# Gated DeltaNet layers of a decoder trunk: order of the inverse's matmuls, place of two sample updates, and the engine that scales one group of query products

## The chip, the cores and the metric

The program runs on one NeuronCore of one Trainium2 chip. Its engines are TensorE (PE in the profile, with PEld for its weight loads), VectorE (DVE), ScalarE (ACT), GpSimd (POOL) and SyncE (SP, which issues DMAs). Each engine works through its own list of instructions in the order in which it was written, and waits at semaphores for the others. The metric is the time of one execution on the device in microseconds (us), median of the runs.

## The reference, cut to what matters

The reference runs a prompt of 256 tokens and a decode batch of 8 sequences with 4 tokens each through four layers. Every layer has a half-step SwiGLU FFN, a token mixer and another half-step FFN. Layers 0 and 3 have a gated DeltaNet mixer with 8 heads of 128; the change lies in it alone. For the prompt it works in four chunks of 64 tokens:

```
a_mat = eye + (kb @ kc^T) * decay_strict          # 64 x 64 for each head and chunk
u, w  = solve(a_mat, [v * beta, kb * exp(gc)])    # unit lower triangular
step(S):  v_new = u_n - w_n @ S                   # four steps, one after the other
          o     = qg_n @ S + attn_n @ v_new
          S     = S * gl_n + kdec_n^T @ v_new
o = rmsnorm(o) * silu(z);  y = o @ w_out
```

The samples have a state of their own for every sequence and head, 8 x 8 matrices of 128 x 128, which gets `S * gl + kdec^T @ v_new` once.

## The kernel before

Everything is float32. Big projections are done as three passes of rounded halves (lines 412 to 414 and 1275 to 1277); the small products of the mixer are plain float32 matmuls. The eight heads are two groups `g` of four, the four chunks two tiles `p` of 128 tokens with two halves `e`. There is no scheduler: each engine's order is written out by hand, and the order of the source is the order of issue. `once(engine, "name", v)` makes an engine wait until the named semaphore has reached v; `.then_inc` raises it when the instruction is done.

**The inverse.** `pe_gdn` inverts the triangular matrices by levels. Level l is `inverse_z(pe, l)` (L1438, 64 matmuls of 64 x 64 into `ZBANK`), then VectorE's `masked_z(l)` (L1998, two instructions), `inverse_x(pe, l)` (L1453, 64 matmuls) and VectorE's `x_turned(l)` (L2004, two transposes) beside ScalarE's `xt_copy`. Each waits for the one before. Between them TensorE does other work: `turned(pe, t)` for t = 0 to 7 turns one tile of keys (t even) or values (t odd) into a bank of PSUM (L1395 for group 0, L1398 for group 1), `sample_small(pe, k)` (L1466, 16 small matmuls) and `sample_old(pe, n, g)` (L1479). VectorE's `k_scaled(t)` (L2016) and ScalarE's `v_scaled(t)` (L1687) read what was turned. All `turned` raise one semaphore, `g_t`.

**The recurrence.** `chain(pe, c)`, c = 0 to 3, is one chunk step: the product of w and S (L1555); VectorE subtracts it from u (L2128, two instructions, `g_y`); the product of q and S (L1566, `g_qs`), which ScalarE scales into `O` (`q_scaled`, L1783, four instructions a group, `g_qe`); the product of the attention and v_new (L1579), which VectorE adds to `O` (L2141, `g_o`); and `chain_state` (L1594), the state's product, which VectorE adds to S (L2120).

**The samples' states.** The 16 updates k = 0 to 15 are products of one 32-row strip each with 512 columns (`sample_update`, L1542). Strip k % 4 is used. Updates 0 to 3 have four PSUM banks, 0, 1, 2 and 6; from k = 4 on `update_bank` is k % 2, so bank 0 or 1. An even update is added to the state by VectorE (`updated(k)`, L2090, raises `g_s_new`). An odd one is copied to `fbuf` by ScalarE (`update_copied(k)`, L1775, raises `g_ssu_copied`) and added by GpSimd (L1186, raises `g_s_odd`). From k = 4 on update k waits first for its bank:

```
once(pe, ("g_s_new", "g_ssu_copied")[k % 2], k // 2)
```

which is `updated(k - 2)` for an even k and `update_copied(k - 2)` for an odd one. In step c > 0 TensorE sends updates 4c and 4c + 1 behind the product of q and S, and 4c + 2 and 4c + 3 at the end of the step.

**The end of the recurrence.** TensorE sends `outputs_turned` 0 to 3 (L1608, L1611), 14 matmuls whose result nobody reads (`pe_filled`, L494), `outputs_turned` 4 and 5, 12 more such matmuls, and then the output projection (L1275). VectorE takes means of squares (`mean(2)`, L2095), gates what was turned (`gated`, L2103, in the order 0, 2, 4, 1, 3, 5) and makes the low parts (`low`, L2110). ScalarE squares (L1755), takes the root (`root(2)`, L1759 and L1760), scales group 0 of `O` (`normed(1, 0)`, L1799) and makes the high parts (`hi`, L1769). `gated(0)` writes where `update_copied(13)` had put its copy, so it waits for seven adds of GpSimd (`g_s_odd`). The projection starts when the low parts 0, 2 and 4 are there.

Of the kernel before, what the change touches and what calls it, by code (L numbers as in the profile page):

```python
# [19 lines left out]
ALU = mybir.AluOpType  # L20
# [37 lines left out]
def tables():  # L58
# [53 lines left out]
    for b in range(NB):  # L112
# [18 lines left out]
        g_evac=14, g_silu=12, g_sq=8, g_ss_half=1, g_act_seq=4, g_lnp=1, g_alog=1, g_egl=1, g_lk=1, g_ce=1, g_trow_ready=2, g_dt=2,  # L131
        g_dts=1, g_tv=4, g_x=10, g_s_x=1, g_s_xt2=1, g_s_y=1, g_ue=4, g_qe=4, g_ms=5, g_ro=3, g_on=3, g_on_d=1, g_on_p=2, g_o_hi=6,
        g_dve_seq=14, g_hist_in=10, g_tap=12, g_tapped=24, g_z_in=4, g_hist=1, g_cbuf_half=2, g_cbuf_set=1, g_conv=12, g_tail=12, g_gate_read=2, g_abs=1, g_gl=1,
        g_rows=2, g_egx=1, g_ssr=1, g_colc=1, g_tabr=1, g_e=1, g_m2=2, g_xt=4, g_tk=4, g_s_xt=1, g_s_kv=2, g_s_r=1, g_s_rhs=1,
# [85 lines left out]
def trunk(nc, a, subs):  # L220
# [29 lines left out]
    def once(eng, name, v):  # L250

        eng.wait_ge(sem(name), v + before(name))

    with ctx:
# [819 lines left out]
        o_cols = lambda k: slice(k * P, (k + 1) * P) if k < 2 else slice(0, 4 * P)  # L1074
        DBANK, KQBANK, ZBANK, XTBANK = ((2, 3), (4, 5)), (6, 7), (2, 6), (7, 3)
        TBANK, UBANK, WBANK = (1, 5, 4, 5, 1, 5, 4, 5), ((2, 4), (3, 7)), ((5, 6), (0, 2))
        SUBANK, QSBANK, AYBANK, OBANK = (4, 5), (2, 6), (3, 7), (2, 2, 4, 6, 3, 7)
# [127 lines left out]
        def pe_gdn(pe, n):  # L1205
# [23 lines left out]
            inverse_z(pe, 2)  # L1229
            sample_turned(pe)  # L1230
            inverse_x(pe, 2)
            sample_small(pe, 0)
            turned(pe, 0)
            turned(pe, 1)
            inverse_z(pe, 3)
            sample_small(pe, 1)
            turned(pe, 2)
            turned(pe, 3)
            inverse_x(pe, 3)
            sample_small(pe, 2)  # L1240
            turned(pe, 4)
            turned(pe, 5)
# [138 lines left out]
        def turned(pe, t):  # L1381

            g, p, v = t // 4, t // 2 % 2, t % 2
            if t == 0:
                once(pe, "g_s_kv", 1)
                once(pe, "g_silu", 12)
            elif t < 3:
# [12 lines left out]
            last.then_inc(sem("g_t"), 1)  # L1400
# [144 lines left out]
        def chain(pe, c):  # L1545

            p, e = c // 2, c % 2
            if c == 0:
                once(pe, "g_ue", 4)
                once(pe, "g_we", 2)  # L1550
            else:
                once(pe, "g_s", 2 * c)
                for hh in range(4):
                    for g in range(2):
                        last = pe.matmul(psum[halves(e ^ g), SUBANK[g], hh * P:(hh + 1) * P], WT[:, g, e, 2 * hh + p, :],  # L1555
                                         S[:, 4 * g + hh, :], start=True, stop=True)
                        if hh == 3:
                            last.then_inc(sem("g_ws"), 1)
                if c == 1:
                    once(pe, "g_s_new", 2)  # L1560
                    once(pe, "g_ssu_copied", 2)
                elif c == 2:
                    once(pe, "g_qe", 2)
                for hh in range(4):
                    for g in range(2):
                        last = pe.matmul(psum[halves(e ^ g), QSBANK[g], hh * P:(hh + 1) * P], q4[:, 0, 4 * g + hh, chunk(p, e)],  # L1566
                                         S[:, 4 * g + hh, :], start=True, stop=True)
                        if e == 1 and hh == 3:
                            last.then_inc(sem("g_qs"), 1)
                sample_update(pe, range(4 * c, 4 * c + 2))  # L1570
                once(pe, "g_y", 2 * c)
# [13 lines left out]
            if c == 3:  # L1585
                chain_state(pe, c)
            sample_update(pe, range(4 * c + 2 * (c > 0), 4 * c + 4))

# [10 lines left out]
        def outputs_turned(pe, k):  # L1599

            p, g = (None, None, 0, 0, 1, 1)[k], k % 2
            if k == 0:
                once(pe, "g_qe", 4)
            elif k == 2:
                once(pe, "g_s", 7)
            once(pe, ("g_on", "g_on", "g_on_p", "g_on_p", "g_on", "g_on_d")[k], (1, 2, 1, 2, 3, 1)[k])
            if p is None:
# [6 lines left out]
        def act_gdn(act, n):  # L1614
# [67 lines left out]
            def v_scaled(t):  # L1682
                g, p = t // 4, t // 2 % 2
                once(act, "g_t", t + 1)
                for hh in range(4):
# [91 lines left out]
            def q_scaled(p):  # L1777
                for g in range(2):
                    once(act, "g_qs", 2 * p + g + 1)
# [44 lines left out]
            q_scaled(1)  # L1824
            update_copied(13)
            squared(1, 0, whole=False)
            squared(1, 1, heads=range(2))
            root(2, slice(8, 16))
            normed(1, 0)
            update_copied(15)  # L1830
            for k in OUT_ORDER:
# [39 lines left out]
        def dve_gdn(dve, n):  # L1871
# [139 lines left out]
            def k_scaled(t):  # L2011
                g, p = t // 4, t // 2 % 2
                once(dve, "g_t", t + 1)
                cols = slice(8 * p + 4 * g, 8 * p + 4 * g + 4)
                for k, dst in ((1, Kb), (2, KD)):
# [32 lines left out]
            dve.tensor_tensor(RHS, two(psum[:, 1, 256:512]), sc(0), ALU.mult).then_inc(sem("g_s_kv"), 1)  # L2048
            x_turned(2)
            masked_z(3)  # L2050
# [3 lines left out]
            once(dve, "g_conv_out", 128)  # L2054
            k_scaled(0)
            x_turned(3)
            k_scaled(2)
            masked_z(4)
# [63 lines left out]
            for c in range(4):  # L2122
                p, e = c // 2, c % 2
                if c > 0:
                    for g in range(2):
                        once(dve, "g_ws", 2 * (c - 1) + g + 1)
                        yv = U[halves(e ^ g), g, p]
                        dve.tensor_tensor(yv, yv, four(psum[halves(e ^ g), SUBANK[g], :]), ALU.subtract).then_inc(sem("g_y"), 1)  # L2128
                    updated(4 * c)
                if c < 3:  # L2130
# [5 lines left out]
                if e == 1:  # L2136
                    for g in range(2):
                        once(dve, "g_ay", 2 * p + g + 1)
                        once(dve, "g_qe", 2 * p + g + 1)
                        rows = slice(0, P) if p else halves(1 - g)  # L2140
# [11 lines left out]
            once(dve, "g_zs", 4)  # L2152
            mean(2, slice(8, 16))
            updated(14)
            state_added(3, 1)
# [1707 lines left out]
```

## Time and profile before

| | us |
|---|---|
| median of 3 runs | 2508.9 (2507.91 to 2509.67) |
| the profiled execution: its own time | 2510.39 |
| its span, first to last instruction | 2508.7 |
| TensorE busy | 2484.8 (99%) |
| VectorE busy | 1566.8 (62%) |
| ScalarE busy | 1187.4 (47%) |
| GpSimd busy | 313.5 (12%) |
| mean granted TensorE clock | 0.999 |

Starts are counted from the first instruction of the span. A row of a timeline has the start, the length of the merged piece, the engine, the line, what is written and read, how many instructions were merged, and in brackets the idle time before them and what ended it. The length of a piece of TensorE runs to the modelled end of its last matmul, so the next piece often starts a little before it; the distance from start to start is the time that a piece takes of the engine.

### The profile page before, as it was taken

Reading aid. Unit: us, or ns where it says so; the run is one execution under the profiler, and the core shown is the slowest. Engines: PE = TensorE matmul, PEld = TensorE weight load, DVE = VectorE, ACT = ScalarE, POOL = GpSimd, SP = SyncE. Lnnn points to the kernel's source line nnn. Section 1 sums busy time; section 2 is a strip of 40 time slices with the busy share of each in tenths; the row PEclk is TensorE's granted clock in tenths of the full one; section 3 lists DMA queues with packets and bytes.
Section 4 is the critical chain, followed back from the end, with each engine's and each line's share of the span. In section 5 each row is a group of like instructions: output and inputs, shape, how many; then the busy total and the mean of one; then the engine's idle time right before and its main releaser. Section 6 shows DMA issues by size and latency. Waiting matters only on the chain.

```text
span 2508.7 us, 49685 instructions
## 1 busy us (share of the span) xinstructions
PE 2484.8 (99%) x20967; PEld 2391.4 (95%) x20967; DVE 1566.8 (62%) x1956; ACT 1187.4 (47%) x1622; POOL 313.5 (12%) x336
## 2 busy tenths in 40 slices
PE   9999999999999999999999999999999999999999
PEld 9999988999999987799999999999999999979999
DVE  5556977755665556575465556675566549867654
ACT  5434755544544455454354444453454437555443
POOL 1001025100100155010010010110020011061000
PEclk9999999999999999999999999999999999999999
DMA  7546535444554657354455465555454466345543
GB/s 226 167 139 179 170 91 171 158 163 143 181 167 142 194 167 223 120 164 159 150 179 167 143 186 185 159 181 163 143 186 162 138 183 172 99 134 169 167 143 112
DMA packets 425365, 404.16 MB, mean 161 GB/s; under 512 B 27996, under 2 KB 420824, under 8 KB 424888
## 3 DMA queue, kind: packets, MB, share of 16 engines
q1 hardware_dynamic: 420568, 392.44, 50.1%
q0 software_dynamic: 4480, 9.18, 1.2%
q8 instruction: 129, 2.11, 0.4%
q14 instruction: 44, 0.36, 0.0%
q10 hardware_dynamic: 144, 0.07, 0.0%
HBM read 385.25 MB, written 16.39 MB: 160 GB/s over the span
## 4 chain that ended last, share of the span: by engine, by line
PE 96%; DVE 2%; issue 1%; ACT 1%; DMA 0%; SPq 0%; DVEq 0%; ACTq 0%
PE psum L412 25%; PE psum L413 25%; PE psum L414 25%; PE psum L750 2%; PE psum L754 2%; PE psum L751 2%; PE psum L3235 1%; PE psum L3248 1%; PE psum L3274 1%; PE psum L1542 1%; PE psum L532 0%; PE psum L507 0%; PE psum L1453 0%; PE psum L1438 0%; PE psum L1579 0%
## 5 line engine op out<-in xcount | busy, mean ns | idle before, releaser
L392 DVE TENSOR_TENSOR w_lo<-raw,w_hi 128x2048 fp32r<-128x2048 f32 (+3 forms) x361 | 742.8, 2058 | 492.4 <-ACT w_hi L375 491.8
L412 PE MATMUL psum<-xn_hi,w_hi 128*128 128x288 f32 x3296 | 974.1, 296 | 0.9 <-issue 0.4
L413 PE MATMUL psum<-xn_lo,w_hi 128*128 128x288 f32 x3296 | 973.3, 295 | 0.0
L414 PE MATMUL psum<-xn_hi,w_lo 128*128 128x288 f32 x3296 | 969.9, 294 | 0.0
L375 ACT ACTIVATE w_hi<-raw 128x2048 fp32r<-128x2048 f32 (+2 forms) x349 | 597.5, 1712 | 771.8 <-PE psum L414 756.9
L412 PEld LDWEIGHTS psum<-xn_hi,w_hi 128*128 128x128 f32 x3296 | 621.3, 189 | 6.9 <-issue 4.4
L414 PEld LDWEIGHTS psum<-xn_hi,w_lo 128*128 128x128 f32 x3296 | 620.1, 188 | 0.0
L413 PEld LDWEIGHTS psum<-xn_lo,w_hi 128*128 128x128 f32 x3296 | 619.4, 188 | 0.7
L413 PE MATMUL psum<-h_lo,w_hi 128*128 128x288 f32 x1408 | 415.5, 295 | 0.0
L414 PE MATMUL psum<-h_hi,w_lo 128*128 128x288 f32 x1408 | 414.9, 295 | 0.0
L412 PE MATMUL psum<-h_hi,w_hi 128*128 128x288 f32 x1408 | 413.2, 293 | 0.0
L414 PEld LDWEIGHTS psum<-h_hi,w_lo 128*128 128x128 f32 x1408 | 264.7, 188 | 0.0
L412 PEld LDWEIGHTS psum<-h_hi,w_hi 128*128 128x128 f32 x1408 | 264.7, 188 | 0.0
L413 PEld LDWEIGHTS psum<-h_lo,w_hi 128*128 128x128 f32 x1408 | 264.6, 188 | 0.0
L473 POOL TENSOR_TENSOR fbuf<-sq 128x576 f32<-128x576 f32 x21 | 42.9, 2041 | 1578.6 <-ACT sq L780 1375.7
L889 ACT ACTIVATE h_hi<-fbuf 128x576 f32 (+1 forms) x88 | 60.4, 687 | 207.2 <-DVE fbuf L953 207.2
L926 DVE TENSOR_TENSOR sg<-psum,rr 128x576 f32<-128x576 f32 x81 | 61.4, 757 | 154.5 <-PE psum L414 153.3
L956 DVE TENSOR_TENSOR h_lo<-fbuf,h_hi 128x576 f32 (+1 forms) x88 | 66.8, 759 | 81.0 <-ACT h_hi L889 81.0
L477 POOL TENSOR_TENSOR fbuf<-fbuf,sq 128x576 f32<-128x576 f32 x30 | 66.7, 2223 | 142.2 <-ACT sq L780 139.6
L1907 DVE SCALAR_TENSOR_TENSOR g_cacc<-g_cbuf,vec,g_cacc 128x312 f32<-128x312 f32 x144 | 73.8, 554 | 1.7
L953 DVE TENSOR_TENSOR fbuf<-sg,fbuf 128x576 f32<-128x576 f32 x88 | 66.2, 752 | 5.0 <-DVE fbuf L946 4.4
L927 DVE TENSOR_TENSOR fbuf<-psum,rr 128x576 f32<-128x576 f32 x81 | 60.6, 748 | 0.0
(673 smaller groups left out, 2906.9 us busy)
## 6 DMA issues: line engine op xcount, KB each, us to landing
raw<-w_ffn_up SPq DMA_DIRECT2D x175, 1024.0 KB, 5.1
raw<-w_ffn_down SPq DMA_DIRECT2D x64, 768.0 KB, 4.5
raw<-w_ffn_down SPq DMA_DIRECT2D x64, 640.0 KB, 4.2
raw<-gdn_w_in SPq DMA_DIRECT2D x32, 1024.0 KB, 5.6
raw<-mlstm_w_in SPq DMA_DIRECT2D x12, 1024.0 KB, 5.4
raw<-gdn_w_out SPq DMA_DIRECT2D x8, 1024.0 KB, 5.3
raw<-cache_mla_latent SPq DMA_DIRECT2D x36, 128.0 KB, 3.7
a_split<-cache_mla_latent SPq DMA_DIRECT2D x36, 128.0 KB, 3.2
```

The source lines that it names most:

```text
L375: act.activation(spread(w_hi[slot(u, i)], u), packed(raw[u % NRAW], u), ACT.Copy).then_inc(hi_ready, 1)
L392: dve.tensor_tensor(spread(w_lo[slot(u, i)], u), packed(raw[u % NRAW], u), spread(w_hi[slot(u, i)], u).bitcast(F32), ALU.subtract).then_in ...
L412: pe.matmul(out, wh[:, k, c], hi(k), start=st, stop=False)
L413: pe.matmul(out, wh[:, k, c], lo(k), start=False, stop=False)
L414: last = pe.matmul(out, wl[:, k, c], hi(k), start=False, stop=sp_)
L477: pool.tensor_tensor(sq_part, sq_part, sq[:, 2 * i:2 * i + 2, :], ALU.add).then_inc(sum_step, 1)
L889: act.activation(dst, fbuf[:, j % 2], ACT.Copy).then_inc(hhi_done, 1)
L926: dve.tensor_tensor(sg[:, j % 2], psum[:, s:s + 2, 0:T], r2, ALU.mult).then_inc(gate_ready, 1)
L927: dve.tensor_tensor(fbuf[:, j % 2], psum[:, s + 2:s + 4, 0:T], r2, ALU.mult).then_inc(pair_read, 1)
L953: dve.tensor_tensor(fbuf[:, j % 2], sg[:, j % 2], fbuf[:, j % 2], ALU.mult).then_inc(h_done, 1)
L956: dve.tensor_tensor(h_lo[:, sl, :], fbuf[:, j % 2], h_hi[:, sl, :].bitcast(F32), ALU.subtract).then_inc(hlo_done, 1)
L1907: last = stt(out=dst, in0=cbuf[:, i % 2, k, j:j + CW - 3], scalar=vec[:, r:r + 1], in1=dst, op0=ALU.mult, op1=ALU.add)
```

## The change

In the inverse, `turned(1)` is sent before `turned(0)`, and both, `turned` 2, 3 and 4, and `sample_small` 0 and 1 get other places between the levels. `k_scaled` and `v_scaled` ask for a tile's place in the new order, `k_scaled(0)` comes before `masked_z(3)`, `k_scaled(2)` before `x_turned(3)`, and the wait for the sum of the silus moves from `turned(0)` to `turned(1)` and `turned(2)`. In the last step of the recurrence TensorE sends updates 12 and 13 together with 14 and 15, behind `chain_state`; `updated(12)` goes behind `mean(2)` and `update_copied(13)` behind `normed(1, 0)`; and group 1 of the query products is scaled by VectorE in one instruction instead of by ScalarE in four. `sample_update` itself, with its banks and waits, is not touched.

```
+        TURN_ORDER = (1, 0, 2, 3, 4, 5, 6, 7)
 ...
             inverse_z(pe, 2)
             sample_turned(pe)
+            sample_small(pe, 0)
+            turned(pe, 1)
             inverse_x(pe, 2)
-            sample_small(pe, 0)
             turned(pe, 0)
-            turned(pe, 1)
+            turned(pe, 2)
+            sample_small(pe, 1)
             inverse_z(pe, 3)
-            sample_small(pe, 1)
-            turned(pe, 2)
             turned(pe, 3)
+            turned(pe, 4)
             inverse_x(pe, 3)
             sample_small(pe, 2)
-            turned(pe, 4)
             turned(pe, 5)
             inverse_z(pe, 4)
 ...  turned(pe, t)
             if t == 0:
                 once(pe, "g_s_kv", 1)
+            elif t < 3:
                 once(pe, "g_silu", 12)
-            elif t < 3:
                 once(pe, "g_dt", 2)
 ...  chain(pe, c)
-                sample_update(pe, range(4 * c, 4 * c + 2))
+                if c < 3:
+                    sample_update(pe, range(4 * c, 4 * c + 2))
                 once(pe, "g_y", 2 * c)
 ...
             if c == 3:
                 chain_state(pe, c)
-            sample_update(pe, range(4 * c + 2 * (c > 0), 4 * c + 4))
+            sample_update(pe, range(4 * c + 2 * (c in (1, 2)), 4 * c + 4))
 ...  outputs_turned(pe, k)
             if k == 0:
-                once(pe, "g_qe", 4)
+                once(pe, "g_qe", 3)
             elif k == 2:
                 once(pe, "g_s", 7)
+            elif k == 3:
+                once(pe, "g_o", 4)
 ...  v_scaled(t) on ScalarE, and the same in k_scaled(t) on VectorE
-                once(act, "g_t", t + 1)
+                once(act, "g_t", TURN_ORDER.index(t) + 1)
 ...  q_scaled(p)
-                for g in range(2):
+                for g in range(2 - p):
 ...  ScalarE's order
             q_scaled(1)
-            update_copied(13)
             squared(1, 0, whole=False)
             squared(1, 1, heads=range(2))
             root(2, slice(8, 16))
             normed(1, 0)
+            update_copied(13)
             update_copied(15)
 ...  VectorE's order in the inverse
             x_turned(2)
+            once(dve, "g_conv_out", 128)
+            k_scaled(0)
             masked_z(3)
 ...
-            once(dve, "g_conv_out", 128)
-            k_scaled(0)
+            k_scaled(2)
             x_turned(3)
-            k_scaled(2)
             masked_z(4)
 ...  VectorE's order in the recurrence
-                    updated(4 * c)
+                    if c < 3:
+                        updated(4 * c)
+                if c == 3:
+                    once(dve, "g_qs", 4)
+                    step(dve.tensor_tensor(O[:, 1, 1], four(psum[:, QSBANK[1], :]), CE[:, 3, 12:16, None].to_broadcast([P, 4, P]),
+                                           ALU.mult))
 ...
-                        once(dve, "g_qe", 2 * p + g + 1)
+                        once(dve, "g_qe", 3 if p else g + 1)
 ...
             mean(2, slice(8, 16))
+            updated(12)
             updated(14)
             state_added(3, 1)
```

## Rows read from the trace of the kernel before

**Rows 1.** The page's part 4: the chain that ended last, by engine.
```profile
PE 96%; DVE 2%; issue 1%; ACT 1%; DMA 0%; SPq 0%; DVEq 0%; ACTq 0%
```

**Rows 2.** Timeline of TensorE, layer 3, last step of the recurrence and after.
```profile
2249.14 1.13 PE L1542 MATMUL psum<-g_ym,y 32*128 32x512 f32 x4
2250.20 1.09 PE L1579 MATMUL psum<-g_u,g_m 64*64 64x128 f32 x16
...
2252.32 1.13 PE L1542 MATMUL psum<-g_ym,y 32*128 32x512 f32 x4
2253.37 0.44 PE L1608 MATMUL psum<-base,g_xn 128*128 128x128 f32 x2
...
2254.44 2.09 PE L494 MATMUL psum<-w_hi 128*128 128x288 f32 x14
2256.37 0.60 PE L1611 MATMUL psum<-base,g_o 128*128 128x128 f32 x4
...
2259.72 0.37 PE L1275 MATMUL psum<-xn_hi,w_hi 128*128 128x288 f32 x1 [0.36 <-DVE xn_lo L2110]
```

**Rows 3.** Timeline of VectorE, the same stretch.
```profile
2248.37 1.40 DVE L2128 TENSOR_TENSOR g_u<-g_u,psum 64x512 f32<-64x512 f32 x2 [0.33 <-PE psum L1555]
2250.30 0.69 DVE L2090 TENSOR_TENSOR y<-y,psum 128x512 f32<-128x512 f32 x1 [0.53 <-PE psum L1542]
2251.32 1.28 DVE L2141 TENSOR_TENSOR g_o<-g_o,psum 128x512 f32<-128x512 f32 x2 [0.33 <-PE psum L1579]
...
2254.16 0.17 DVE L2095 SCALAR_TENSOR_TENSOR g_ms<-g_ms,g_qe 128x8 f32<-128x8 f32 x1
...
2255.47 0.34 DVE L2103 SCALAR_TENSOR_TENSOR fbuf<-psum,vec,g_z 128x128 f32<-128x128 f32 x1
...
2257.01 0.75 DVE L2103 SCALAR_TENSOR_TENSOR g_ft<-psum,vec,g_z 128x512 f32<-128x512 f32 x1
```

**Rows 4.** Timeline of ScalarE, the same stretch.
```profile
2249.31 2.18 ACT L1783 ACTIVATE g_o<-psum,g_ce 128x128 f32<-128x128 f32 x8 [0.98 <-PE psum L1566]
...
2254.85 1.29 ACT L1799 ACTIVATE g_o<-g_o,g_ro 128x128 f32<-128x128 f32 x4
2256.04 0.58 ACT L1775 ACTIVATE fbuf<-psum 128x512 f32<-128x512 f32 x1
```

**Rows 5.** Timeline of GpSimd, the same stretch.
```profile
2252.05 1.28 POOL L1186 TENSOR_TENSOR y<-y,fbuf 128x512 f32<-128x512 f32 x1 [0.15 <-ACT fbuf L1775]
```

**Rows 6.** Timeline of TensorE, layer 3, step 0: four updates in a row.
```profile
2233.25 1.14 PE L1542 MATMUL psum<-g_ym,y 32*128 32x512 f32 x8
```

**Rows 7.** Timeline of TensorE, layer 3, the solved products.
```profile
2219.72 1.96 PE L1519 MATMUL psum<-g_vb,g_xt 64*64 64x128 f32 x32 [0.35 <-DVE g_xt L2009]
...
2224.55 0.84 PE L1498 MATMUL psum<-sq,g_xts 32*32 32x128 f32 x16 [0.93 <-DVE sq L2077]
2225.32 3.39 PE L1519 MATMUL psum<-g_vb,g_xt 64*64 64x128 f32 x32
```

**Rows 8.** Windows: busy time of each engine, PEclk (granted clock), DMA share.
```profile
2226.00:2228.00 2.00, 2.00 (x24) 2.00 (x22) 0.00 (x0) 0.60 (x1) 2.00 (x2) 0.50 0.03 11
```

**Rows 9.** Timeline of TensorE, layer 0, the inverse.
```profile
356.41 1.16 PE L1453 MATMUL psum<-g_xt,fbuf 64*64 64x64 f32 x64 [0.61 <-DVE fbuf L1998]
...
357.76 1.09 PE L1395 MATMUL psum<-base,g_qkv 128*128 128x128 f32 x8
358.96 1.16 PE L1438 MATMUL psum<-g_x,g_b 64*64 64x64 f32 x64
...
361.23 0.25 PE L1466 MATMUL psum<-g_xs,g_bs 32*32 32x32 f32 x3 [0.86 <-issue]
...
369.17 1.15 PE L1453 MATMUL psum<-g_xt,fbuf 64*64 64x64 f32 x61 [0.20 <-issue]
...
373.17 0.68 PE L1438 MATMUL psum<-g_x,g_b 64*64 64x64 f32 x29 [0.23 <-issue]
```

**Rows 10.** Timeline of VectorE, layer 0, the inverse.
```profile
357.59 1.31 DVE L2004 STREAM_TRANSPOSE g_x<-psum 128x512 f32<-128x512 f32 x2 [0.67 <-PE psum L1453]
```

More of the change, by code:

```diff
@@ L1230, in pe_gdn @@
             sample_turned(pe)
+            sample_small(pe, 0)
+            turned(pe, 1)
             inverse_x(pe, 2)
-            sample_small(pe, 0)
             turned(pe, 0)
-            turned(pe, 1)
+            turned(pe, 2)
+            sample_small(pe, 1)
             inverse_z(pe, 3)
-            sample_small(pe, 1)
-            turned(pe, 2)
             turned(pe, 3)
+            turned(pe, 4)
             inverse_x(pe, 3)
             sample_small(pe, 2)
-            turned(pe, 4)
             turned(pe, 5)
@@ L1385, in turned @@
                 once(pe, "g_s_kv", 1)
+            elif t < 3:
                 once(pe, "g_silu", 12)
-            elif t < 3:
                 once(pe, "g_dt", 2)
@@ L1569, in chain @@
                             last.then_inc(sem("g_qs"), 1)
-                sample_update(pe, range(4 * c, 4 * c + 2))
+                if c < 3:
+                    sample_update(pe, range(4 * c, 4 * c + 2))
                 once(pe, "g_y", 2 * c)
@@ L1586, in chain @@
                 chain_state(pe, c)
-            sample_update(pe, range(4 * c + 2 * (c > 0), 4 * c + 4))
+            sample_update(pe, range(4 * c + 2 * (c in (1, 2)), 4 * c + 4))
         def chain_state(pe, c):
@@ L1602, in outputs_turned @@
             if k == 0:
-                once(pe, "g_qe", 4)
+                once(pe, "g_qe", 3)
             elif k == 2:
                 once(pe, "g_s", 7)
+            elif k == 3:
+                once(pe, "g_o", 4)
             once(pe, ("g_on", "g_on", "g_on_p", "g_on_p", "g_on", "g_on_d")[k], (1, 2, 1, 2, 3, 1)[k])
@@ L1683, in v_scaled @@
                 g, p = t // 4, t // 2 % 2
-                once(act, "g_t", t + 1)
+                once(act, "g_t", TURN_ORDER.index(t) + 1)
                 for hh in range(4):
@@ L1777, in q_scaled @@
             def q_scaled(p):
-                for g in range(2):
+                for g in range(2 - p):
                     once(act, "g_qs", 2 * p + g + 1)
@@ L1824, in act_gdn @@
             q_scaled(1)
-            update_copied(13)
             squared(1, 0, whole=False)
@@ L1829, in act_gdn @@
             normed(1, 0)
+            update_copied(13)
             update_copied(15)
@@ L2012, in k_scaled @@
                 g, p = t // 4, t // 2 % 2
-                once(dve, "g_t", t + 1)
+                once(dve, "g_t", TURN_ORDER.index(t) + 1)
                 cols = slice(8 * p + 4 * g, 8 * p + 4 * g + 4)
@@ L2049, in dve_gdn @@
             x_turned(2)
+            once(dve, "g_conv_out", 128)
+            k_scaled(0)
             masked_z(3)
@@ L2053, in dve_gdn @@
                               gt("slevel")[:, None, :].to_broadcast([P, 2, NS]), ALU.mult).then_inc(sem("g_s_r"), 1)
-            once(dve, "g_conv_out", 128)
-            k_scaled(0)
+            k_scaled(2)
             x_turned(3)
-            k_scaled(2)
             masked_z(4)
@@ L2128, in dve_gdn @@
                         dve.tensor_tensor(yv, yv, four(psum[halves(e ^ g), SUBANK[g], :]), ALU.subtract).then_inc(sem("g_y"), 1)
-                    updated(4 * c)
+                    if c < 3:
+                        updated(4 * c)
+                if c == 3:
+                    once(dve, "g_qs", 4)
+                    step(dve.tensor_tensor(O[:, 1, 1], four(psum[:, QSBANK[1], :]), CE[:, 3, 12:16, None].to_broadcast([P, 4, P]),
+                                           ALU.mult))
                 if c < 3:
@@ L2153, in dve_gdn @@
             mean(2, slice(8, 16))
+            updated(12)
             updated(14)
```

7 lines of the change are left out of this document (4 added, 3 removed).

## The prediction

> **What bounds the kernel now.** I read the chain that ended last first. TensorE is 96% of it [rows 1], so a time changes only where TensorE comes to wait, loses a wait, or runs at a lower clock. Then the timelines of TensorE around the two places of the change, and those of VectorE, ScalarE and GpSimd for what releases it. The last step of the recurrence is gapless on TensorE up to the output projection, which waits 0.36 us for VectorE's low part [rows 2]. The inverse has short waits, for VectorE and for nothing that the profile shows ("issue") [rows 9]. Layers 0 and 3 run the same code, so each cost counts twice; the tail of layer 0 has the same distances as that of layer 3.
>
> **The last step: updates 12 and 13 moved.** Their place was 2249.14 to 2250.20, 1.06 us, beside VectorE's subtraction, 2248.37 + 1.40 = 2249.77 [rows 2, 3]. The attention product needs that subtraction. With the updates gone it can start 0.1 after 2249.77 instead of at 2250.20, 0.33 earlier. VectorE's add came 1.12 after it (2250.20 to 2251.32), and all up to `mean(2)` (2254.16) hangs on that add, so `mean(2)` comes at 2253.83.
>
> What stands behind this is the point of the forecast. Four updates are now in a row at the end, but `sample_update` keeps its two banks: update 14 waits for `updated(12)`, update 15 for `update_copied(13)`. The change puts `updated(12)` behind `mean(2)` on VectorE and `update_copied(13)` behind `normed(1, 0)` on ScalarE. TensorE keeps its order, so `outputs_turned` 0 to 3, the 14 unread matmuls, `outputs_turned` 4 and 5 and the projection queue up behind update 15. Step by step, in the times of layer 3:
> - `updated(12)`: 2253.83 + 0.1, and 0.69 long [rows 3] = 2254.65. Update 14 goes at 2254.75. From an update's start to VectorE is 1.16 (2249.14 to 2250.30 [rows 2, 3]): VectorE, which stands at `updated(14)`, goes on at 2255.9. Its idle 1.2 us is on nobody's path, since update 15 is later.
> - `normed(1, 0)` began 0.69 after `mean(2)` (2254.16 to 2254.85) and the next copy 1.19 after that, 0.58 long [rows 4]. New: 2253.83 + 0.69 + 1.19 + 0.58 = 2256.29.
> - Update 15 goes at 2256.4. Four updates in four strips took 1.14 [rows 6], two took 1.13 [rows 2]: strips run side by side, so one alone costs the same, 1.05 from start to start. `outputs_turned(0)` starts at 2257.45. It was 2253.37: **+4.1 us**. If the next instruction need not wait for all of a lone update, half of 1.05 goes away: +3.6.
> - From there TensorE's own work goes on as before: 1.07 to the unread matmuls, 1.93 more to `outputs_turned(4)` (2253.37, 2254.44, 2256.37), 0.64 to `gated(4)` (2257.01), 2.71 to the projection (2259.72) [rows 2, 3]. All of it moves by 4.1, and the projection with it. The 0.36 wait at its head was part of that distance and stays.
>
> Hidden behind this: GpSimd's add of update 13 (1.28 [rows 5]) ends at 2256.3 + 1.3 = 2257.6, before `gated(0)`, which needs `outputs_turned(1)` and comes at 2257.9 (2255.47 before [rows 3]). If turning came earlier, this add would bound it, 0.3 behind. Update 15's own copy and add end before `gated(1)`. `updated(12)` (0.69 of VectorE) lies in VectorE's wait.
>
> **The last step: VectorE scales group 1.** ScalarE's eight instructions took 2.18 [rows 4]; four go, 1.09 less. VectorE gets one of 128 x 512, which I price at 0.69 like `updated` [rows 3]: 2249.77 to 2250.45. VectorE waits until 2251.0 for the attention product anyway, so it costs nothing; the cover left is 0.5 us. ScalarE's 1.09 gives nothing either: its squares wait for VectorE's add, and `mean(2)` for VectorE's own squares.
>
> **The inverse.** `inverse_x(2)` stood 0.61 for `masked_z(2)` [rows 9]. Now `sample_small(0)` and a turned tile (half of the eight transposes' 1.20, 357.76 to 358.96) lie there, and the wait is gone. But the loop of `inverse_x(2)`, `x_turned(2)` and `inverse_z(3)` has a length of its own: 356.41 to 358.96, 2.55, the transposes ending at 358.90 [rows 9, 10]. What is left to fill it leaves a wait of 0.1 to 0.2, as before. One half tile (16 matmuls) fewer lies between `inverse_x(3)` and `inverse_z(4)`, where `x_turned(3)` will be waited for, 0.1 to 0.2. `k_scaled(0)` ahead of `masked_z(3)` just fits into VectorE's wait (1.25 of 128 x 512 work in about 1.2). Sum: -0.6 + 0.1 = **-0.5 us** a layer.
>
> The bounds are wider because of "issue". TensorE stood 0.86, 0.20 and 0.23 us for nothing that the profile shows, and the last two pieces end exactly 128 matmuls apart (369.17 to 373.17) [rows 9]. So such a wait sits at a fixed count of instructions, and reordering puts other matmuls there. If the 0.86 falls beside VectorE's work it goes: -1.4. If it falls into the loop, with VectorE standing too, nearly all comes on top: +0.4. I take -0.5, since the 0.61 has a row and the rest has no sign.
>
> **The clock.** In layer 3, after TensorE had stood 0.93 us, the granted clock was 0.50, the 1.2 GHz level, and 32 matmuls took 3.39 us where the same 32 had taken 1.96 [rows 7, 8]: 1.43 lost. Layer 0 has the same code without a fall. The new tail is thinner than that: from 2253.05 to 2257.45 TensorE has two lone updates of one strip each, and stands 1.7 and 0.6 us. I expect the clock to fall there in both layers, and update 15, the transposes and the unread matmuls to run in it: 1.4 a layer, from 0 (no fall) to 2.8 (twice the stretch). For one fall more or less, 1.4.
>
> A rule of the Trainium skill speaks against my price of the moved updates. TensorE: Matmul & The Clock Gate, Part 3 (The mechanism), says that matmuls in different row groups run together in the array. Rows 6 agree: four in 1.14. By it updates 12 to 15 would cost together what two cost, and 1.06 a layer would be won. That needs four banks, which only updates 0 to 3 have.
>
> **Sum.** 2 x (4.1 + 1.4 - 0.5) = +10.0 us. The profiled execution took 2510.39 with a span of 2508.7; it would take 2520.4. The median of the runs was 1.5 lower, 2508.9: forecast **2518.9 us**, +0.40%.
>
> **Rivals.**
> - *No fall of the clock, or in one layer.* For it: none in layer 0 now, and the unread matmuls follow soon. Against it: no stretch before was that thin. 2 x (4.1 - 0.5) = +7.2, 2516.1; with one fall 2517.5.
> - *The wait is shorter.* A lone update takes half, and the inverse wins its bound: 2 x (3.6 - 1.4) = +4.4, 2513.3 without a fall. For it: the inverse's 0.86; against: both have to come together.
> - *Faster: the four updates run side by side.* Place: the end of step 3; price: 1.06 saved there and 0.5 in the inverse, a layer, -3.1, 2505.8. It decides if update 14 does not wait for `updated(12)`. Against it is the line of `sample_update` with k // 2, which is not changed. Nearly excluded. It is what the page's rule above would give.
> - *Same: the delay is absorbed.* It would need slack between the turned outputs and the projection; the only one is the 0.36 wait, which hangs on the same chain. With the lower price and the inverse's bound, +4.4, this is just within 0.2%.
>
> **Chances.** 0.2%, about what a measurement of this kernel can tell from no change, is 5.0 us. Fall in both layers 0.50, in one or none 0.34: both slower. Shorter wait or absorbed, around +4.4: 0.12, of which 0.08 is within 0.2%. Side by side, or another gain: 0.04, half of it beyond 0.2%. Slower 0.88, same 0.10, faster 0.02. Range: below 2 x (3.6 - 1.4) = +4.4, 2513.3; above 2 x (4.1 + 2.8 + 0.4) = +14.6, 2523.5.
>
> **What would show it.** On TensorE, after `chain_state` of step 3, a pair of updates, a wait of about 1.7 us released by VectorE L2090, one update, a wait of about 0.6 released by ScalarE's copy, one update, and only then L1608, about 4 us later behind the state's product than before. VectorE idle ahead of `updated(14)`. The projection's first matmul 16.9 us after the subtraction of step 3 began, 15.5 at full clock (11.35 before, 2248.37 to 2259.72). A granted clock under 1 in two windows of that stretch. `inverse_x(2)` without a wait for L1998. The forecast is wrong if L1608 follows the four updates within 1.2 us, or if the clock stays at 1 in both layers.

## The result, and the profile after

| | before | after |
|---|---|---|
| median of the runs, same chip | 2508.15 (2506.89 to 2509.67, 6 runs) | 2520.81 (2518.55 to 2522.28, 6 runs) |
| ratio, 95% interval | | 1.005 (1.0039 to 1.006) |
| the profiled execution: time, span | 2510.39, 2508.7 | 2518.55, 2516.8 |
| mean granted TensorE clock | 0.999 | 0.997 |

The change costs +12.7 us where +10.0 was forecast; 2520.81 lies in the range. One run of experiment 8 (2681.81 us at a granted clock of 0.851) fell in a slower state and is left out of that experiment's figures. The profiled execution of after is the fastest of its six, so its trace shows +8.1 of span.

The chain that ended last in the kernel after, by engine, beside [rows 1]:

```profile
PE 96%; DVE 2%; ACT 1%; issue 1%; DMA 0%; SPq 0%; DVEq 0%; ACTq 0%
```

The page doesn't show the change at all: shares of the whole span are too coarse for 4 us in two places. The timeline of TensorE does. Line numbers are a few higher in the changed kernels: `sample_update` is L1543 to L1545 instead of L1542, `outputs_turned` L1612 and L1615 instead of L1608 and L1611. After, layer 0: VectorE's subtraction of step 3, then TensorE to the end of the last step (start, length, engine, line, tiles, count, idle before and its releaser):

```profile
405.30 1.40 DVE L2132 TENSOR_TENSOR g_u<-g_u,psum 64x512 f32<-64x512 f32 x2 [0.34 <-PE psum L1556]
```

```profile
406.76 1.09 PE L1581 MATMUL psum<-g_u,g_m 64*64 64x128 f32 x16 [0.61 <-DVE g_u L2132]
...
408.87 1.13 PE L1543 MATMUL psum<-g_ym,y 32*128 32x512 f32 x4
411.65 1.09 PE L1543 MATMUL psum<-g_ym,y 32*128 32x512 f32 x2 [1.65 <-DVE y L2094]
413.30 1.09 PE L1543 MATMUL psum<-g_ym,y 32*128 32x512 f32 x2 [0.56 <-ACT fbuf L1779]
414.32 0.67 PE L1612 MATMUL psum<-base,g_xn 128*128 128x128 f32 x2
...
416.35 2.74 PE L494 MATMUL psum<-w_hi 128*128 128x288 f32 x14
418.93 1.03 PE L1615 MATMUL psum<-base,g_o 128*128 128x128 f32 x8
...
421.87 0.37 PE L1276 MATMUL psum<-xn_hi,w_hi 128*128 128x288 f32 x1 [0.32 <-DVE xn_lo L2114]
```

The reader is to see the queue: one pair of updates, a wait for VectorE's `updated(12)`, one update, a wait for ScalarE's copy, one update, and everything else behind them. `outputs_turned(0)` (L1612) stands 5.45 behind the first update of this row of four; in [rows 2] it stood 1.05 behind the last pair. The same in layer 3, from update 15 on:

```profile
2257.79 2.04 PE L1543 MATMUL psum<-g_ym,y 32*128 32x512 f32 x2 [0.55 <-ACT fbuf L1779]
2259.76 0.69 PE L1612 MATMUL psum<-base,g_xn 128*128 128x128 f32 x2
...
2261.81 3.27 PE L494 MATMUL psum<-w_hi 128*128 128x288 f32 x14
2264.91 1.04 PE L1615 MATMUL psum<-base,g_o 128*128 128x128 f32 x8
...
2267.85 0.37 PE L1276 MATMUL psum<-xn_hi,w_hi 128*128 128x288 f32 x1 [0.32 <-DVE xn_lo L2114]
```

Here update 15 took 1.97 from start to start and the unread matmuls 3.10, against 1.02 and 2.58 in layer 0 and 1.93 before. Windows show why (length; busy time of PE, PEld, DVE, ACT, POOL; then granted clock, DMA share, GB/s), first one of layer 0, then one of layer 3:

```profile
416.00:418.00 2.00, 2.00 (x11) 2.00 (x10) 1.24 (x2) 0.63 (x1) 0.38 (x1) 0.55 0.93 284
...
2258.00:2260.00 2.00, 2.00 (x3) 0.49 (x4) 0.56 (x1) 0.13 (x1) 0.99 (x1) 0.50 0.40 124
...
2262.00:2264.00 2.00, 2.00 (x10) 2.00 (x10) 0.69 (x2) 0.63 (x1) 0.00 (x0) 0.50 0.93 284
```

The clock is at its lower level, 1.2 GHz, for one stretch in layer 0 and for about twice as long in layer 3: added up from windows of 1 us, 3.4 and 6.8 us. VectorE in layer 3 and, at the end, layer 0:

```profile
2251.13 0.68 DVE L2137 TENSOR_TENSOR g_o<-psum,g_ce 128x512 f32<-128x512 f32 x1
...
2255.31 0.69 DVE L2094 TENSOR_TENSOR y<-y,psum 128x512 f32<-128x512 f32 x1
2257.28 0.69 DVE L2094 TENSOR_TENSOR sq<-sq,psum 128x512 f32<-128x512 f32 x1 [1.28 <-PE psum L1543]
...
420.23 0.28 DVE L2114 TENSOR_TENSOR xn_lo<-fbuf,xn_hi 128x128 fp32r<-128x128 f32 x1
```

**Where the 8.1 us of span went.** Distances, each from the rows of both traces:

| | layer 0 | layer 3 |
|---|---|---|
| up to the first state product of the recurrence (layer 3: from layer 0's projection on) | -0.40 | -3.39 |
| subtraction of step 3 to `outputs_turned(0)`: 5.00 before | 9.02: +4.02 | 9.96: +4.96 |
| from there to `outputs_turned(4)`: 3.00 before | 4.61: +1.61 | 5.15: +2.15 |
| from there to the projection: 3.35 before | 2.94: -0.41 | 2.94: -0.41 |

From the first state product to the subtraction both kernels take 17.24. Layer 0 gives +4.8, layer 3 +3.3, and behind it nothing is left over. The -3.39 of layer 3 holds the fall of the clock that [rows 7, 8] showed at 2225 and that is not there after (1.43), 1.8 less of waits of the kind "issue", 0.4 less of waits for VectorE, and +0.36 drift between the layers. The fall comes and goes with the execution: of the eleven traces of this document only that of the kernel before has it. The other kernels with the old order of the inverse have a layer 3 that is about 2 shorter than this one (experiment 1); against such a layer the pair would stand at about +10.

### The profile page after: what moved, and what is told of

The parts are those of the page before. It is cut to its first block, busy times and chain, and to the rows that moved or that the text cites. A ratio compares the mean times of both kernels' runs of the same rounds, so it can differ in the third digit from the quotient of the medians.

```text
span 2516.8 us, 49683 instructions
## 1 busy us (share of the span) xinstructions
PE 2489.7 (99%) x20967; PEld 2393.7 (95%) x20967; DVE 1567.8 (62%) x1958; ACT 1185.5 (47%) x1614; POOL 313.1 (12%) x336
## 4 chain that ended last, share of the span: by engine, by line
PE 96%; DVE 2%; ACT 1%; issue 1%; DMA 0%; SPq 0%; DVEq 0%; ACTq 0%
PE psum L412 25%; PE psum L413 25%; PE psum L414 25%; PE psum L750 2%; PE psum L754 2%; PE psum L751 2%; PE psum L3245 1%; PE psum L3258 1%; PE psum L1543 1%; PE psum L3284 1%; PE psum L1439 0%; PE psum L532 0%; PE psum L507 0%; PE psum L1454 0%; PE psum L1581 0%
```

## The experiments

Each ratio is against the kernel before on the same chip; us in brackets are the difference of the two medians.

**1. The inverse alone.** The new order of `turned`, `sample_small`, `k_scaled` and their waits, on the kernel before; the last step untouched.

```
+        TURN_ORDER = (1, 0, 2, 3, 4, 5, 6, 7)
 ...  the inverse's lines of the change, nothing of the recurrence's
```

> The new order of the inverse alone, the recurrence as before. Theory Q (the whole loss is updates 14 and 15 waiting in TensorE's queue, and the clock that falls over it): no loss here; TensorE reaches the first state product about 0.4 us earlier in layer 0, and in layer 3 0.4 earlier plus 1.4 if the fall of the clock there goes: -0.5 to -2.5 us against before. Rival I (the median 4 us above the profiled run comes from instruction waits in the reordered inverse): +1 to +4 us.

Measured: 1.0003 (0.9994 to 1.0012), 11 runs against 16 [+0.9]. The interval is -1.5 to +3.0 us: theory Q's larger gains are excluded, but the -1.0 that the prediction had for two layers is not, and neither is no change. The wait of `inverse_x(2)` for `masked_z(2)` is gone, as worked out. But TensorE of this kernel, layer 0:

```profile
361.31 0.34 PE L1439 MATMUL psum<-g_x,g_b 64*64 64x64 f32 x8 [0.92 <-issue]
...
366.72 1.15 PE L1439 MATMUL psum<-g_x,g_b 64*64 64x64 f32 x60 [0.62 <-issue]
...
370.52 1.15 PE L1454 MATMUL psum<-g_xt,fbuf 64*64 64x64 f32 x61 [0.52 <-issue]
```

From the first of these waits to the second lie exactly 128 matmuls. Of [rows 9] the 0.86, 0.20 and 0.23 became 0.92, 0.62 and 0.52: +0.77, against the 0.61 saved, and the 0.86, which had fallen into `sample_small`, now falls into `inverse_z(3)`, on whose end VectorE waits. That the new order made the waits longer is not shown by this pair, since their lengths differ between executions of the same order: ahead of the same matmul of the old order the kernel before waits 0.86, and the kernels of experiments 2, 9 and 10 wait 0.30, 0.53 and 0.67. So a wait sits at a count of instructions, and the order decides into which piece it falls.

All traces together say more. From the first matmul of `inverse_z(1)` to the first state product, in us:

| | layer 0 | layer 3 |
|---|---|---|
| old order: before, experiments 2, 9, 10 | 41.22 to 41.90, median 41.44 | 42.12 to 44.89, median 42.88 |
| new order: after, experiments 1, 3 to 7 | 41.50 to 43.97, median 42.10 | 40.19 to 41.38, median 41.14 |

The new order loses 0.7 in layer 0 and wins 1.7 in layer 3, where the waits fall on other matmuls: -1.1 together, an estimate from single executions that the timed runs of this experiment can't tell from 0.

The Trainium skill, Runtime: NRT & Kernel Launch, section Instruction fetch mechanics, has instructions refilled in blocks of 256 and the cost of a crossing "mostly hidden". 128 matmuls with their weight loads (the trace has one for each) are 256 instructions, which agrees; no view shows the refill itself, and the 0.52 to 0.92 us are not hidden.

**2. The last step alone.** The kernel after with the inverse as before.

```
-        TURN_ORDER = (1, 0, 2, 3, 4, 5, 6, 7)
 ...  the inverse's lines taken back, the recurrence's kept
```

> The new last step alone, the inverse as before. Theory Q: the whole loss stays, 5.2 us for a layer with one stretch at the lower clock and 6.7 with two, so +10.4 to +13.4 us against before, some 1 to 2 above the changed kernel's. Rival I: clearly less than the changed kernel's +12.7.

Measured: 1.0057 (1.0043 to 1.0071), 5 runs [+13.0]. Within the measurement the whole loss is in the last step. In layer 0 updates 14 and 15 have the same waits, 1.65 and 0.56. In layer 3 the clock is low already at update 14, behind the wait of 1.65 alone: updates 14 and 15 take 3.62 from start to start, and the second wait has vanished under them.

**3. The copy earlier.** On the kernel after, `update_copied(13)` ahead of the root, so that update 15 is released with update 14.

```
+            update_copied(13)
             root(2, slice(8, 16))
             normed(1, 0)
-            update_copied(13)
             update_copied(15)
```

> The changed kernel with ScalarE's copy of update 13 ahead of root(2) instead of behind normed(1, 0). Theory Q: update 15 now needs only VectorE's updated(12), goes beside update 14, and the turned outputs start about 1.6 us earlier (7.4 us after the subtraction of step 3 instead of 9.0); the wait ahead of it shrinks to the 1.65 one, and at most one stretch at the lower clock is left: +4 to +7 us against before. Rival V (VectorE's two waits, 1.28 and 1.05, are the path, not the copy): less than 1 us better than the changed kernel.

Measured: 1.004 (1.0026 to 1.0054), 5 runs [+10.0]. Less was won than expected: the turned outputs start 8.45 behind the subtraction instead of 7.4. TensorE, layer 0:

```profile
412.34 2.16 PE L1543 MATMUL psum<-g_ym,y 32*128 32x512 f32 x4 [1.65 <-DVE y L2094]
414.44 0.69 PE L1612 MATMUL psum<-base,g_xn 128*128 128x128 f32 x2
...
416.48 3.28 PE L494 MATMUL psum<-w_hi 128*128 128x288 f32 x14
...
422.54 0.37 PE L1276 MATMUL psum<-xn_hi,w_hi 128*128 128x288 f32 x1 [0.32 <-DVE xn_lo L2114]
```

The two updates go together and the second wait is gone. But the pair takes 2.1 where a pair takes 1.06 at full clock, the same matmuls of the next stages 0.69 and 3.28 where they took 0.44 and 2.09: both layers now have the long stretch at the lower clock, and the projection of layer 0 stands 16.55 behind the subtraction, no earlier than in the kernel after (16.57). The windows of this kernel (columns as above):

```profile
410.00:422.00 12.00, 10.35 (x52) 8.17 (x48) 6.72 (x14) 5.48 (x20) 2.54 (x2) 0.72 0.70 209
2254.00:2266.00 12.00, 10.14 (x50) 8.47 (x51) 6.72 (x15) 4.79 (x16) 2.54 (x2) 0.72 0.73 219
```

**4. The waits filled.** On the kernel after, 11 and 4 unread matmuls in the two waits, so that the engine works through them.

```
 ...  the end of chain(pe, 3)
+            sample_update(pe, range(12, 14))
+            once(pe, "g_qe", 3)
+            pe_filled(pe, u0 + 17, 2, 11)
+            sample_update(pe, range(14, 15))
+            pe_filled(pe, u0 + 17, 2, 4)
+            sample_update(pe, range(15, 16))
```

> The changed kernel with unread matmuls (11 and 4 of 128x288) in TensorE's two waits, ahead of update 14 and ahead of update 15; nothing else moves. Theory Q with the clock as a part of its own: both waits stay in place and length (the subtraction of step 3 to the turned outputs 9.0 us), but the granted clock stays 1, so 1.6 us go in layer 0 and 3.1 in layer 3: about +8 us against before (+7 to +9). Rival C (the clock does not matter, its stretches lie beside waits): as the changed kernel, +12.

Measured: 1.0031 (1.0019 to 1.0043), 6 runs [+7.5]. TensorE of layer 0, and a window of the same stretch:

```profile
410.55 1.71 PE L494 MATMUL psum<-w_hi 128*128 128x288 f32 x11
412.27 1.09 PE L1543 MATMUL psum<-g_ym,y 32*128 32x512 f32 x2
413.30 0.80 PE L494 MATMUL psum<-w_hi 128*128 128x288 f32 x4
414.02 1.12 PE L1543 MATMUL psum<-g_ym,y 32*128 32x512 f32 x2
```

```profile
406.00:423.00 17.00, 16.06 (x129) 12.69 (x125) 12.96 (x24) 8.82 (x30) 6.01 (x6) 1.00 0.49 148
```

This parts the two costs. Updates 14 and 15 go no earlier than in after. In both layers the projection stands 15.08 behind the subtraction, against 11.35 before: 2 x 3.73 = 7.5, and the time is +7.5. The clock stays at 1.00 in both tails, and 5.2 us of the 12.7 are gone, though matmuls were added. So the wait costs 7.5 and the clock about 5. Each of the two times is known to some 3 us, but the traces agree: behind the subtraction the projection stands 1.5 and 3.0 later in the kernel after than here, 1.5 and 2.3 in experiment 2, 2.6 and 3.1 in experiment 7, so 3.8 to 5.7 for two layers.

**5. Another order of TensorE, same banks.** On the kernel after, `outputs_turned` 0 to 3 ahead of update 14, and update 15 behind the unread matmuls.

```
             for k in range(4):
                 outputs_turned(pe, k)
+            sample_update(pe, range(14, 15))
             once(pe, "g_o", 3)
             pe_filled(pe, u0 + 17, 3, 14)
+            sample_update(pe, range(15, 16))
             for k in range(4, 6):
                 outputs_turned(pe, k)
```

> The changed kernel with TensorE's order alone changed: outputs_turned 0 to 3 ahead of update 14, the 14 unread matmuls behind it, then update 15, then outputs_turned 4 and 5. Banks, waits and the other engines' orders are as in the changed kernel. Theory Q (what costs is what queues behind the two waits on TensorE): turned outputs start 4.6 us after the subtraction of step 3 instead of 9.0, the second wait is covered by the unread matmuls, the projection starts 13.3 after the subtraction at full clock instead of 15.1, now bound by update 15 and by GpSimd's add of update 13 ahead of gated(0); fewer stretches at the lower clock: +3 to +6 us against before. Rival V (VectorE's order is the path: updated(12) behind mean(2), and then its wait for update 14): the projection not earlier than 15 after the subtraction, +8 or more.

Measured: 1.0019 (1.001 to 1.0028), 11 runs [+5.0], as expected, though not by the expected rows. TensorE, then VectorE, layer 0:

```profile
410.69 0.44 PE L1614 MATMUL psum<-base,g_xn 128*128 128x128 f32 x2
...
412.42 1.09 PE L1545 MATMUL psum<-g_ym,y 32*128 32x512 f32 x2 [0.41 <-DVE y L2096]
...
420.12 0.37 PE L1278 MATMUL psum<-xn_hi,w_hi 128*128 128x288 f32 x1 [0.88 <-DVE xn_lo L2116]
```

```profile
415.33 0.35 DVE L2109 SCALAR_TENSOR_TENSOR fbuf<-psum,vec,g_z 128x128 f32<-128x128 f32 x1 [0.50 <-POOL y L1187]
...
417.89 0.87 DVE L2116 TENSOR_TENSOR xn_lo<-fbuf,xn_hi 128x128 fp32r<-128x128 f32 x1
```

`outputs_turned(0)` is back at 4.63 behind the subtraction, yet the projection is 14.06 behind it, where 13.3 was expected. The bound that the prediction had put "0.3 behind" now rules: `gated(0)` waits for GpSimd's add of update 13, and the low part takes 0.87 instead of 0.28. In layer 0 TensorE also waits 1.16 behind the projection, by the store that experiment 6 shows. The clock is 1.00 in both tails.

**6. Four banks.** On the kernel after, updates 14 and 15 in banks 3 and 7, the copy early as in experiment 3, and the unread matmuls in bank 0.

```
-        update_bank = lambda k: (0, 1, 2, 6)[k] if k < 4 else k % 2
+        update_bank = lambda k: (0, 1, 2, 6)[k] if k < 4 else (3, 7)[k - 14] if k > 13 else k % 2
 ...  sample_update(pe, ks), for k = 14 and 15
+                    once(pe, "g_o", 4)
```

> The changed kernel with banks 3 and 7 for updates 14 and 15 (they wait for the last add to O instead of for updates 12 and 13), the copy of update 13 ahead of root(2), and the unread matmuls in bank 0. Theory Q: both waits are gone, the four updates run side by side in at most 1.5 us, turned outputs start 5.1 to 5.3 us after the subtraction (5.0 before), the projection 11.2 to 11.5 after it (11.35 before), the clock stays: what is left is the inverse, -1 to +2 us against before. Rival V: VectorE's chain is 0.6 longer by updated(12), so +1.2 from the recurrence alone, +2 or more.

Measured: 1.0013 (1.0004 to 1.0022), 11 runs [+3.3]: missed, -1 to +2 was expected. The four updates run without a wait for their banks, but there is no gain. Layer 0, TensorE, VectorE beside it, and ScalarE behind the tail:

```profile
409.48 1.74 PE L1545 MATMUL psum<-g_ym,y 32*128 32x512 f32 x8
411.16 0.44 PE L1614 MATMUL psum<-base,g_xn 128*128 128x128 f32 x2
...
415.83 0.41 PE L1617 MATMUL psum<-base,g_o 128*128 128x128 f32 x2 [1.08 <-DVE g_o L2172]
```

```profile
414.15 1.53 DVE L2172 TENSOR_TENSOR g_o<-g_o,g_ro 128x512 f32<-128x512 f32 x1
```

```profile
422.34 1.92 ACT L375 ACTIVATE w_hi<-raw 128x2048 fp32r<-128x2048 f32 x1 [2.35 <-DMA gdn_S_s<-sq]
```

Two new losses are in it. VectorE's scaling of `O`, 0.68 in the kernel after, takes 1.53 beside GpSimd's add, and TensorE waits 1.08 for it; the projection stands 11.98 behind the subtraction in both layers, 0.63 later than before. In the kernel before the scaling started 0.31 ahead of that add and was through in 0.68 (layer 3, VectorE and GpSimd; the row behind it is the low part 0 beside the same add):

```profile
2256.39 0.68 DVE L2160 TENSOR_TENSOR g_o<-g_o,g_ro 128x512 f32<-128x512 f32 x1
...
2257.67 0.70 DVE L2110 TENSOR_TENSOR xn_lo<-fbuf,xn_hi 128x128 fp32r<-128x128 f32 x1
```

```profile
2256.70 1.53 POOL L1186 TENSOR_TENSOR sq<-sq,fbuf 128x512 f32<-128x512 f32 x1 [3.37 <-ACT fbuf L1775]
```

The other stands behind the projection: ScalarE's next `w_hi` waits for a store of the samples' states, 2.35 here and 1.04 in layer 3, and through it and VectorE TensorE stands 2.23 and 0.93. The kernel before has no such wait. 2 x 0.63 + 2.23 + 0.93 = 4.4; the profiled execution was 4.5 above the median of before.

**7. ScalarE scales both groups.** The kernel after, with the query products' scaling as before, and the counts of its semaphores with it.

```
-                for g in range(2 - p):
+                for g in range(2):
```

> The changed kernel with ScalarE scaling both groups of the query products as before. Theory Q (the edit is worth nothing as long as ScalarE waits for VectorE's add): within 1 us of the changed kernel, +11.5 to +13.5 against before. Rival S (ScalarE's 1.1 us fewer bring its squares, root and copy of update 13 forward): 1 to 2 us a layer worse than the changed kernel.

Measured: 1.0047 (1.0033 to 1.0061), 5 runs [+13.0; after itself +12.7]. The times, known to some 3 us, don't part theory Q from rival S, but the trace does: from the attention product of step 3 to updates 14 and 15 it has 4.88 and 6.53 in both layers, against 4.89 and 6.54 in the kernel after. ScalarE's freed time brought neither update forward. The windows of both tails (columns as above):

```profile
411.00:425.00 14.00, 12.03 (x63) 8.58 (x61) 7.60 (x16) 6.37 (x24) 3.10 (x3) 0.76 0.58 176
2255.00:2269.00 14.00, 11.75 (x66) 8.37 (x67) 6.46 (x12) 7.29 (x29) 4.66 (x5) 0.76 0.48 145
```

A mean of 0.76 over 14 us is 6.7 us at the lower level, the long stretch, in both layers.

**8 and 9. Four banks, inverse as before, the last state sum later.** Experiment 6 with the old inverse, VectorE's last `state_added` behind the low parts, and 10 unread matmuls for 14.

```
             updated(14)
-            state_added(3, 1)
 ...
                 low(k)
+            state_added(3, 1)
```

> The kernel with four banks, the inverse in its old order, the last state sum of group 1 behind all low parts on VectorE, and 10 unread matmuls instead of 14 ahead of outputs_turned 4. Theory Q: projection 10.7 to 10.9 after the subtraction of step 3 instead of 11.35, so -0.9 to -1.3 us against before, if the clock stays. Rival: fewer unread matmuls let the clock fall or the projection's second half waits for VectorE: 0 to +3.

Measured: 1.0014 (1.0005 to 1.0023), 11 runs [+4.0]: missed. The same kernel again, for its trace:

> A second look at the kernel with four banks, the inverse as before, the last state sum behind the low parts and 10 unread matmuls, for its trace: its time was +3.5 us over the kernel before where -0.9 to -1.3 was expected. Theory S (a new bound behind the tail): the projection starts 11 to 12 us behind the subtraction in both layers, and the loss is a wait of ScalarE's L375 for the store of the state (gdn_S_s), 1 to 3 us, which VectorE and TensorE then wait for in turn. Theory T (the tail itself): the projection starts 12.5 us or more behind the subtraction, because TensorE's turned outputs wait for VectorE. Theory C: the granted clock is under 1 in one of the two tails.

One execution, 2508.65, 1.0 above the median of before on that chip. TensorE, VectorE, GpSimd and ScalarE, layer 0:

```profile
414.09 0.63 PE L1616 MATMUL psum<-base,g_o 128*128 128x128 f32 x4 [1.59 <-DVE g_o L2170]
...
416.16 0.38 PE L1275 MATMUL psum<-xn_hi,w_hi 128*128 128x288 f32 x1
...
423.98 0.40 PE L412 MATMUL psum<-xn_hi,w_hi 128*128 128x288 f32 x1 [1.24 <-DVE w_lo L392]
```

```profile
412.22 1.72 DVE L2170 TENSOR_TENSOR g_o<-g_o,g_ro 128x512 f32<-128x512 f32 x1
```

```profile
412.13 1.26 POOL L1186 TENSOR_TENSOR sq<-sq,fbuf 128x512 f32<-128x512 f32 x1 [0.87 <-ACT fbuf L1780]
```

```profile
419.61 1.92 ACT L375 ACTIVATE w_hi<-raw 128x2048 fp32r<-128x2048 f32 x1 [1.36 <-DMA gdn_S_s<-sq]
```

Both parts are there, as in experiment 6. The projection starts 11.97 behind the subtraction, 0.6 a layer later than before, for the same stretched instruction (1.72). And ScalarE waits 1.36 for a store of the samples' states, then VectorE and in the end TensorE, 1.24 in layer 0 and 0.87 in layer 3. 2 x 0.6 + 1.24 + 0.87 = 3.3, near the +4.0 of the timed runs, though this one execution was only 1.0 above. Theory S holds with T's cause beside it; the clock was 1.00.

The later sum of the state is not what makes the store late: experiment 6 has the wait without the later sum, experiment 10 the later sum without the wait. What both kernels with the wait share is that the tail's four stores of the samples' states go out within 3 us of each other in layer 0, instead of within 7 before, and that the slowest lands after 7.2 us (experiment 6) and 6.2 (here), instead of 3.4. That the crowding is the cause is not shown; experiment 5 has a wait of 1.28 with its stores 6 us apart and a slowest landing of 5.2.

**10. The kernel before with the last state sum later**, and 10 unread matmuls for 14; nothing else.

> The kernel before, with VectorE's last sum of the state (0.68 us) moved from ahead of gated(0) to behind the last low part, and 10 unread matmuls instead of 14 in the first group. Theory Q (the queue in front of the output projection is what the time hangs on): gated(0) comes up to 0.6 earlier on VectorE, the low part 0, which took 0.70 beside GpSimd's add of update 15 where 0.28 is its length alone, falls less into that add, and TensorE's own four unread matmuls are 0.55 less. The projection starts 0.6 to 1.0 us earlier behind the subtraction (11.35 before, 10.4 to 10.8 now) in both layers: -1.2 to -2.0 us in all, if the clock stays up. Rival R (the time of the tail is VectorE's and GpSimd's shared work, whatever its order): GpSimd's add stretches other VectorE work by as much, projection 0 to 0.3 earlier, 0 to -0.6 us. Rival C (the clock): with fewer unread matmuls the granted clock falls in one of the two stretches, +1 to +3 us.

Measured: 0.9996 (0.9987 to 1.0005), 11 runs against 15 [-1.0]. The time alone would fit theory Q as well as rival R; the rows decide for R. VectorE, then TensorE, layer 0:

```profile
414.13 0.57 DVE L2110 TENSOR_TENSOR xn_lo<-fbuf,xn_hi 128x128 fp32r<-128x128 f32 x1
```

```profile
412.77 1.09 PE L1611 MATMUL psum<-base,g_o 128*128 128x128 f32 x8 [0.19 <-ACT g_o L1799]
...
416.05 0.37 PE L1275 MATMUL psum<-xn_hi,w_hi 128*128 128x288 f32 x1 [0.60 <-DVE xn_lo L2110]
```

The projection comes 11.09 behind the subtraction, 0.25 earlier a layer, and the low part still takes 0.57. TensorE now waits 0.19 for `normed` and 0.60 for the low part: the tail hangs on ScalarE and VectorE, and no version here beats the kernel before beyond the measurement.

## Why the prediction was right, point by point

- *The pair's gap.* Right: the attention product follows VectorE's subtraction at once (0.61 idle in TensorE), and VectorE's add 1.18 later. `mean(2)` came 5.41 behind the subtraction, against 5.79 before: 0.38 gained where 0.33 was forecast. `outputs_turned(0)` would have had it too, had it not been queued.
- *Update 14 waits for `updated(12)`, update 15 for the copy.* Right, 1.7 and 0.6 forecast, 1.65 and 0.56 measured. It rested on one line of the code that the change leaves alone, and on counting what stands ahead of the releasers.
- *A lone update costs what four cost.* Right: 1.02 in layer 0 at full clock (413.30 to 414.32), 1.03 and 1.05 in experiment 4.
- *+4.1 at `outputs_turned(0)`.* Right: +4.02 in layer 0; in layer 3 +4.96, of which 0.95 is update 15 at the lower clock. "All of it moves by 4.1, and the projection with it" was 0.4 too much: update 15's place moved GpSimd's second add off the low part 0, which took 0.28 instead of 0.70. At full clock the forecast had the projection 15.5 behind the subtraction, experiment 4 has 15.08.
- *The scaling.* Right: VectorE's 0.68 lies in its wait, and ScalarE's freed time is worth nothing (experiment 7).
- *The inverse, -0.5 a layer.* Open: by time +0.9 (-1.5 to +3.0) for two layers where -1.0 was forecast (experiment 1). The named wait went. By the traces the sum of about -1.1 fits the forecast, but not its way: +0.7 in layer 0 and -1.7 in layer 3, both outside the bounds of -1.4 to +0.4 that were to hold for a layer. "The rest has no sign" did not hold: the waits of the kind "issue" fell on other matmuls in either layer, and the prediction worked from those of layer 0 alone. If the sum is right, luck had a part in it.
- *The clock, 1.4 a layer.* The mechanism was right, the size was not: this is the term that was mis-sized. One stretch cost 1.61, two cost 3.1 (0.95 in update 15 and 2.15 behind it), and by experiment 4 the clock is about 5 us in all instead of 2.8; the bound of 2.8 a layer would have held it. Of eight tails with the waits unfilled (after, experiments 2, 3 and 7) six have the long stretch and two, both of layer 0, the short one. That most executions of after have it in both layers would explain why they lie 1.3 to 3.7 above the profiled one; no trace of such a run of after was taken.
- *The sum.* The forecast had 8.2 for the wait, 2.8 for the clock and -1.0 for the inverse. The medians give 7.5, 5.2 and about 0, so +10.0 for +12.7 holds two errors of opposite sign, 0.7 too much for the wait and 2.4 too little for the clock, beside a third term that the times can't tell from 0.
- *The Trainium skill's rule* (TensorE: Matmul & The Clock Gate, Part 3 (The mechanism)), that different row groups run together: [rows 6] agree, four in 1.07 from start to start. With four banks at the end (experiment 6) the four took 1.68, against 5.45 with two. The 1.06 a layer that the rival priced were not there to win: the pair's old place lay beside VectorE's subtraction, and only 0.38 of it was on the path, while the last pair's place grew from 1.05 to 1.68. `outputs_turned(0)` came 5.25 behind the subtraction, against 5.00 before.
- *The rivals.* No fall of the clock: excluded by the windows, and 7.5 is what it would have been (7.2 forecast). The shorter wait: excluded, since a lone update took 1.02 and not half of it. Side by side and absorbed: excluded by the rows of the two waits and of the projection, 5.22 and 6.70 later in the two layers.

## What to carry to other kernels

When instructions move behind others on an in-order engine, list for each the semaphore it waits for and where its releaser now stands in its own queue; a wait at the head of a queue costs its length for all that follows, here 4 us a layer for 0.38 us of gap saved. Price the clock with the wait: filling the same wait with work that nobody reads won 5 of 12.7 us without starting any needed instruction earlier. And before giving a tail more resources, look what is next: here another order and four banks each uncovered waits for another engine or a store, of 0.4 to 2.2 us of TensorE.

## What the runs showed of the hardware

- VectorE beside GpSimd: with both inputs in SBUF, 128x512 took 1.53 and 1.72 instead of 0.68, and 128x128 0.57 to 0.87 instead of 0.28, while GpSimd added 128x512 (1.26 to 1.53). In each of the five cases (before, experiments 5, 6, 9 and 10, layer 0) VectorE's instruction ended 0.54 to 0.55 (128x512) or 0.14 to 0.15 (128x128) after GpSimd's add had ended. So by these rows it was held until the add was through, rather than slowed throughout. `gated`, which reads PSUM, kept its 0.75 inside such an add (2257.01 in [rows 3], inside GpSimd's 2256.70 + 1.53). The Trainium skill, GPSIMD Engine Reference, section 1. Specifications, says that the SBUF interface is shared with VectorE's instructions of two SBUF inputs; the rows agree.
- Waits for "issue" in runs of small matmuls stand a fixed count apart, 128 matmuls where one follows on the next, and differ in length between executions: 0.30 to 0.86 us ahead of one and the same matmul, 0.20 to 1.48 over all of the inverse.
- After waits of 1.65 and 0.56 around one lone update the clock fell to 1.2 GHz in both layers of after and in layer 0 of experiment 2; after the 1.65 alone it fell in both layers of experiment 3 and in layer 3 of experiment 2. With 11 and 4 matmuls in the same waits it fell in neither layer. A wait alone does not decide: in layer 3, ahead of the second half of the solved products, the fall came in the kernel before (0.93) and not in after (0.96), experiment 1 (0.95) and experiment 2 (1.23).
